# A mixer layer behind an in-projection: the units of the projection in another order, a 32x32 solve beside the last five of them, and one product in two halves

## The chip, the core and the metric

The kernel runs on one core of a Trainium2 chip. The metric is the time of one execution on the device in microseconds (us), median of several runs. The core's engines work from queues of their own and meet at semaphores: TensorE (PE) does matrix products into eight PSUM banks, VectorE (DVE) and ScalarE (ACT) do elementwise work and read PSUM, GpSimd (POOL) does elementwise work on SBUF, and SyncE (SP) issues the transfers. Each queue is worked through in order.

## The reference

Two blocks on 512 tokens of width 1024, all in float32. The first is a Fourier mix and a gated convolutional feed-forward. The second is a feed-forward, a mixer, and a feed-forward. The change lies in the mixer of the second block. Cut to it:

```python
p = rms_norm_2(x, mix_norm) @ w_in                    # 512 x 2208: r, k, v, w, a, g and 512 pooling inputs
p_rw = p_rw + (token_shift(p_rw) - p_rw) * mu_shift   # all but the pooling inputs
p_r, p_k, p_v, p_w, p_a, p_g = split(p_rw)
decay = exp(-exp(-softplus(-(w0 + tanh(p_w) @ w_lora_up)) - 0.5))
a = sigmoid(a0 + p_a @ a_lora_up)
g = sigmoid(p_g) @ g_lora_up
kk = p_k * k_k / norm_per_head(p_k * k_k)
k = p_k * (1 + (a - 1) * k_a)
# for each head (64 wide), one token after the other:
sa = state @ -kk
state = state * w + outer(sa, kk * a) + outer(v, k)
y = state @ r
y = group_norm(y) * ln_w + ln_b + sum(r * k * r_k) * v
out = concat([y * g, multiscale_pool_mix(p_pool)]) @ w_out
```

## The kernel before, in words

**Weights.** All large weights come as 233 units of 128x1024 floats through a ring of four slots. SP loads a unit into `raw`, ACT rounds it into `w_hi` (`high`, the copy at L623), POOL subtracts to get `w_lo` (`low`, four pieces of 128x256 at L459), and PE multiplies: eight blocks of three matmuls (`three`, L1568 to L1570), 24 for a unit.

**In-projection.** There are 18 units (`IN_ORDER`), 128 output channels each: `wa` (inputs of the decay and of `a`), `gx` (input of the gate), four of keys `k`, four of receptances `r`, four of values `v`, four of pooling inputs. Four PSUM banks are used in turn. Behind each unit PE does `small_products(i)`, DVE scales the bank into `pads` (`normed`), ACT takes its share of the token shift (`own_share`, L772) and DVE adds the other (`shifted`). Elementwise work on keys, decays and receptances is put by hand, by `if i == ...`, behind one unit or another in the four engines' programs. The names used below: `decay` (a scan and a subtraction), `key_sums` and `key_norms` (norms per head), `key_scale` and `key_unit` (the norms spread and applied), `removal(p)` (three DVE operations that make kk and kk*a with the decays in; p is one of four pairs of heads), `receptance(p)` (two), `triangle_grams(p)` (L1807, on PE, needs `removal(p)`), `tri_out(p)` (ACT copies the 32x32 diagonal blocks to `tri_g`, and others to `off`), `bonus_product` (L1813, needs `receptance`).

**The solve.** The recurrence is worked out in chunks of 64 tokens; that needs inverses of unit lower triangular 32x32 blocks, for all heads and chunks at once. `triangles()` on DVE is a generator: a transpose into `tri_m`, then 31 steps of a product into `tri_p` and an addition into `tri_x`, each waiting for the one before, then a transpose back into `tri_t`. `solve_steps(n)` issues n pieces of it (the first transpose is one).

**Pairs.** Two pairs of heads are worked at a time on two sets of buffers. `in_turns` writes the order: the even lane's first four pieces (up to `yield`), the odd lane's first four, ten more of the even lane, and then one of each in turn. A pair: four transposes (`tA` to `tV`, copied out by ACT), `LR` (masked by DVE at L1402), `K0` and `K1` (masked by DVE at L1407), `AV` (L1911, the masked keys times the values, copied out by ACT), then `G1` (L1922), `W` (L1929), `GH` (L1935) and more, and a scan `S1` to `S6` over the chunks (L1978 on PE, L1454 on DVE in turn). `G1` needs `TT`, four ACT copies of `tri_t` (L907), which stand in ACT's queue behind the copy of `AV`. PE's first transposes wait for `in_done`, which DVE gives at L1375, in its queue behind the solve steps of the in-projection.

## Time and profile before

| | us |
|---|---|
| median of 3 runs | 1612.47 (1611.6 to 1615.66) |
| the profiled execution, whole | 1617.07 |
| its span, first to last instruction | 1615.3 |
| busy in it: PE, POOL, DVE, ACT | 1509.5, 758.7, 560.2, 510.0 |

The in-projection takes the span from 880 to 1020 us, the pairs from 1022 to 1182. PE is busy for 93% of the span; the two stretches around 985 and from 1013 to 1060 us are those in this part where it is not. The granted clock of PE is given as a share of 2.4 GHz, and it has two levels, 1.2 and 2.4 GHz.

### The profile page before, as it was taken

Reading aid. Unit: us, or ns where it says so; the run is one execution under the profiler, and the core shown is the slowest. Engines: PE = TensorE matmul, PEld = TensorE weight load, DVE = VectorE, ACT = ScalarE, POOL = GpSimd, SP = SyncE. Lnnn points to the kernel's source line nnn. Section 1 sums busy time; section 2 is a strip of 40 time slices with the busy share of each in tenths; the row PEclk is TensorE's granted clock in tenths of the full one; section 3 lists DMA queues with packets and bytes.
Section 4 is the critical chain, followed back from the end, with each engine's and each line's share of the span. In section 5 each row is a group of like instructions: output and inputs, shape, how many; then the busy total and the mean of one; then the engine's idle time right before and its main releaser. Section 6 shows DMA issues by size and latency. Waiting matters only on the chain.

```text
span 1615.3 us, 20178 instructions
## 1 busy us (share of the span) xinstructions
PE 1509.5 (93%) x7230; PEld 1248.7 (77%) x7230; DVE 560.2 (35%) x790; ACT 510.0 (32%) x706; POOL 758.7 (47%) x1013
## 2 busy tenths in 40 slices
PE   5787999999999999999999999688888999999997
PEld 5675888888887788888887787577766888888887
DVE  6695342222004722222003546834434322222003
ACT  4424333333124332223124563122223323222212
POOL 0363464555555664455545544250025655445553
PEclk9888999999999999999999999779889999999999
DMA  8871234232231232322332221000012332232321
GB/s 308 313 261 40 92 131 147 100 100 96 92 103 65 92 117 91 104 91 92 103 101 69 95 79 40 1 1 1 1 53 91 105 104 91 91 104 92 103 78 53
DMA packets 44545, 156.90 MB, mean 97 GB/s; under 512 B 4944, under 2 KB 7376, under 8 KB 44240
## 3 DMA queue, kind: packets, MB, share of 16 engines
q1 hardware_dynamic: 44496, 156.22, 28.0%
q8 instruction: 33, 0.54, 0.1%
q14 instruction: 16, 0.13, 0.0%
HBM read 154.11 MB, written 2.10 MB: 97 GB/s over the span
## 4 chain that ended last, share of the span: by engine, by line
PE 81%; DVE 12%; ACT 3%; issue 3%; DMA 1%; POOL 1%; SPq 0%; DVEq 0%; ACTq 0%; POOLq 0%
PE ps L1568 24%; PE ps L1569 24%; PE ps L1570 24%; DVE mod_acc L1028 2%; DVE act_lo L1028 1%; PE ps L1922 1%; DVE hid_lo L1028 1%; PE ps L1911 1%; DVE tri_p L1025 1%; DVE tri_x L1025 1%; DVE xT L1028 1%; DVE MK L1407 1%; PE ps L1982 1%; PE ps L1581 1%; DVE act_lo L1025 1%
## 5 line engine op out<-in xcount | busy, mean ns | idle before, releaser
L459 POOL TENSOR_TENSOR w_lo<-raw,w_hi 128x256 fp32r<-128x256 f32 x932 | 692.7, 777 | 773.4 <-ACT w_hi L623 773.3
L1568 PE MATMUL ps<-act_hi,w_hi 128*128 128x512 f32 x1328 | 529.9, 399 | 19.2 <-DVE act_lo L1025 10.8
L1569 PE MATMUL ps<-act_lo,w_hi 128*128 128x512 f32 x1328 | 521.7, 393 | 0.0
L1570 PE MATMUL ps<-act_hi,w_lo 128*128 128x512 f32 x1328 | 520.9, 392 | 0.0
L623 ACT ACTIVATE w_hi<-raw 128x1024 fp32r<-128x1024 f32 x233 | 245.0, 1055 | 452.1 <-PE ps L1570 426.0
L1568 PEld LDWEIGHTS ps<-act_hi,w_hi 128*128 128x128 f32 x1328 | 252.3, 190 | 83.6 <-issue 13.5
L1569 PEld LDWEIGHTS ps<-act_lo,w_hi 128*128 128x128 f32 x1328 | 252.4, 190 | 53.5 <-issue 2.6
L1570 PEld LDWEIGHTS ps<-act_hi,w_lo 128*128 128x128 f32 x1328 | 252.2, 190 | 53.2
L1568 PE MATMUL ps<-hid_hi,w_hi 128*128 (+3 forms) x584 | 220.2, 377 | 10.8 <-DVE hid_lo L1028 7.3
L1569 PE MATMUL ps<-hid_lo,w_hi 128*128 (+3 forms) x584 | 219.6, 376 | 0.0
L1570 PE MATMUL ps<-hid_hi,w_lo 128*128 (+3 forms) x584 | 219.5, 376 | 0.0
L1568 PEld LDWEIGHTS ps<-hid_hi,w_hi 128*128 128x128 f32 x584 | 110.9, 190 | 31.0 <-issue 11.5
L1570 PEld LDWEIGHTS ps<-hid_hi,w_lo 128*128 128x128 f32 x584 | 110.9, 190 | 19.8
L1569 PEld LDWEIGHTS ps<-hid_lo,w_hi 128*128 128x128 f32 x584 | 110.9, 190 | 19.7
L718 ACT ACTIVATE hid_hi<-g_buf 128x512 f32 (+1 forms) x66 | 41.8, 633 | 257.9 <-DVE g_buf L1168 217.6
L1165 DVE TENSOR_TENSOR u_buf<-ps,rstd 128x512 f32<-128x512 f32 x44 | 30.4, 691 | 182.6 <-PE ps L1570 182.6
L1170 DVE TENSOR_TENSOR hid_lo<-g_buf,hid_hi 128x512 f32 (+1 forms) x66 | 48.2, 730 | 58.7 <-ACT hid_hi L718 58.7
L1163 DVE TENSOR_TENSOR g_buf<-ps,rstd 128x512 f32<-128x512 f32 x44 | 30.4, 691 | 93.9 <-PE ps L1570 93.5
L716 ACT ACTIVATE g_buf<-g_buf 128x512 f32<-128x512 f32 x66 | 41.1, 622 | 48.9 <-DVE g_buf L1155 37.3
L1153 DVE SCALAR_TENSOR_TENSOR g_buf<-ps,vec,g_buf 128x511 f32<-128x511 f32 x22 | 16.5, 750 | 106.6 <-ACT g_buf L714 106.6
L1028 DVE SCALAR_TENSOR_TENSOR xT<-ps,mods,xT 128x512 f32<-128x512 f32 x16 | 12.0, 751 | 115.9 <-PE ps L1570 115.5
L1533 DVE SCALAR_TENSOR_TENSOR xT<-ps,xT 128x256 f32<-128x256 f32 x16 | 6.8, 425 | 110.0 <-PE ps L1570 110.0
(262 smaller groups left out, 1175.0 us busy)
## 6 DMA issues: line engine op xcount, KB each, us to landing
raw<-weight_units SPq DMA_DIRECT2D x233, 512.0 KB, 3.2
wm_ring<-mod_units SPq DMA_DIRECT2D x16, 512.0 KB, 6.4
wm_mid<-mod_units SPq DMA_DIRECT2D x16, 512.0 KB, 7.1
wm_early<-mod_units SPq DMA_DIRECT2D x8, 512.0 KB, 9.5
wm_late<-mod_units SPq DMA_DIRECT2D x8, 512.0 KB, 5.3
x_tok<-tokens SPq DMA_DIRECT2D x4, 512.0 KB, 5.4
xT<-tokens_by_channel SPq DMA_DIRECT2D x1, 2048.0 KB, 16.4
result<-act_out SPq DMA_DIRECT2D x16, 128.0 KB, 1.8
```

The source lines that it names most:

```text
L459: ins = nc.gpsimd.tensor_tensor(w_lo[:, slot, c], raw[:, slot, c], w_hi[:, slot, c].bitcast(f32), SUB)
L623: nc.scalar.activation(w_hi[:, slot, :], raw[:, slot, :], ACT.Copy).then_inc(hi_done, 1)
L716: nc.scalar.activation(g_buf[:, q, :], g_buf[:, q, :], ACT.Silu).then_inc(s["silu"], 1)
L718: nc.scalar.activation(hid_hi[:, bass.ds(j * T, T)], g_buf[:, q, :], ACT.Copy).then_inc(s["hid_hi"], 1)
L1025: chain(nc.vector.tensor_tensor(o, a, b, op), name)
L1028: chain(nc.vector.scalar_tensor_tensor(o, a, s, b, op0, op1), name)
L1163: nc.vector.tensor_tensor(g, gate, rstd[:, :], MUL).then_inc(s["act_in"], 1)
L1165: nc.vector.tensor_tensor(u_, val, rstd[:, :], MUL).then_inc(s["val_read"], 1)
L1170: nc.vector.tensor_tensor(hid_lo[:, bass.ds(j * T, T)], g, hid_hi[:, bass.ds(j * T, T)].bitcast(f32), SUB).then_inc(s["hid_lo"], 1)
L1568: nc.tensor.matmul(o, wh, xh, start=start, stop=False, **check)
L1569: nc.tensor.matmul(o, wh, xl, start=False, stop=False, **check)
L1570: return nc.tensor.matmul(o, wl, xh, start=False, stop=stop, **check)
```

## The change

Four things move or are cut, and no operation is taken away:

1. `IN_ORDER` puts the four key units first, two value units, the receptances around one pooling unit, two value units, and three pooling units last. The small work follows: the grams stand behind units 10 and 11 (before, 12 and 13), the last receptances behind unit 13 (before, 17).
2. The solve's steps stand behind units 13 to 17 (5, 6, 6, 6, 6 pieces), and the rest in one piece ahead of pair 0's first mask. None is left between the masks of pairs 0 and 1.
3. `AV` becomes `AVa` (two chunks, needs only K0's masks) and `AVb` (needs K1's); ACT copies out the first half and DVE the second.
4. POOL's own order: `tri_x` is set up ahead of the low parts of units 12 to 14, the four products `key_in` stand ahead of those of units 15 to 17 (before, all low parts came first).

```diff
-IN_ORDER = [("wa", 0), ("gx", 0), ("k", 0), ("k", 1), ("pool", 0), ("k", 2), ("k", 3), ("pool", 1), ("r", 0), ("v", 0), ("r", 1), ("v", 1),
-            ("r", 2), ("v", 2), ("r", 3), ("v", 3), ("pool", 2), ("pool", 3)]
+IN_ORDER = [("wa", 0), ("gx", 0), ("k", 0), ("k", 1), ("k", 2), ("k", 3), ("v", 0), ("v", 1), ("r", 0), ("r", 1), ("pool", 0), ("r", 2),
+            ("r", 3), ("v", 2), ("v", 3), ("pool", 1), ("pool", 2), ("pool", 3)]
...
-            low_through(U_IN + AHEAD - 1, U_OUT)
+            low_through(U_IN + AHEAD - 1, U_IN + 12)
...
+            low_through(U_IN + 12, U_IN + 15)
             for p in range(PAIRS):
                 pool.wait_ge(sem("removed"), p + 1)
                 nc.gpsimd.tensor_tensor(rK[:, p, :], rBonus[:, p, :], rK[:, p, :], MUL).then_inc(sem("key_in"), 1)
+            low_through(U_IN + 15, U_OUT)
...
-                copy("AV", b.AA[:, :, :, HS:P], 2, "q (c h k) -> q c h k", c=NCP, h=2)
+                pe_did("AVa")
+                did("AVa", nc.scalar.activation(b.AA[:, 0:2, :, HS:P], ps[:, b.bank + 2, 0:HALF].rearrange("q (c h k) -> q c h k", c=2, h=2), ACT.Copy))
...
+                if i == 9:
+                    removal(0)
+                    removal(1)
                 if i == 10:
-                    for q in range(PAIRS):
-                        key_unit(q)
-                    removal(0)
-                if i == 11:
-                    removal(1)
+                    receptance(0)
                     removal(2)
+                    removal(3)
                 if i == 13:
-                    receptance(1)
-                if i == 14:
-                    solve_steps(4)
-                if i == 15:
+                    receptance(2)
+                    receptance(3)
+                    solve_steps(5)
+                if i >= 14:
                     solve_steps(6)
-                if i == 16:
-                    receptance(2)
-                    solve_steps(4)
-                if i == 17:
-                    receptance(3)
-                    solve_steps(4)
...
-                if p < 2:
-                    solve_steps(5)
                 if p == 0:
+                    solve_steps(SB)
                     for q in range(PAIRS):
                         bonus(q)
...
                 keys(0, 2)
-                if p < 2:
-                    solve_steps(2)
                 yield
                 keys(1, 0)
                 yield
+                pe_did("AVb")
+                did("AVb", nc.vector.tensor_copy(b.AA[:, 2:4, :, HS:P], ps[:, b.bank + 3, 0:HALF].rearrange("q (c h k) -> q c h k", c=2, h=2)))
                 yield
...
-                if i == 12:
+                if i == 10:
                     triangle_grams(0)
                     triangle_grams(1)
-                if i == 13:
+                if i == 11:
                     triangle_grams(2)
                     triangle_grams(3)
...
                 keys(1, 0)
+
+                def values(half):
+                    for c in (0, 1) if half == "a" else (2, 3):
+                        for h in range(2):
+                            last = nc.tensor.matmul(bank(2 + c // 2)[:, (c % 2 * 2 + h) * HS:(c % 2 * 2 + h + 1) * HS], b.MK[:, 1, c, h, :], b.VT[:, c * P + h * HS:c * P + (h + 1) * HS], start=True, stop=True)
+                    did(f"AV{half}", last)
+
+                ve_did("K0b")
+                values("a")
                 yield
                 ve_did("K1b")
-                for c in range(NCP):
-                    for h in range(2):
-                        last = nc.tensor.matmul(bank(2)[:, (2 * c + h) * HS:(2 * c + h + 1) * HS], b.MK[:, 1, c, h, :], b.VT[:, c * P + h * HS:c * P + (h + 1) * HS], start=True, stop=True)
-                did("AV", last)
+                values("b")
```

**DVE at the end of the in-projection and at pair 0.** First the kernel before, from solve step 20 on; `rBonus<-ps,rV` is `bonus`, `MBR` and `MK` are the masked `LR` and keys of pair 0.

```order
L1025 TENSOR_TENSOR tri_x<-tri_x,tri_p 128x10x22
L1025 TENSOR_TENSOR rBonus<-ps,rV 128x512 x4
L1402 TENSOR_TENSOR MBR_120<-ps,sumsq 128x4x128 x2
L1407 TENSOR_TENSOR MK_121<-ps,sumsq 128x2x2x128 x2
L1025 TENSOR_TENSOR tri_p<-tri_x,tri_m 128x207
L1025 TENSOR_TENSOR tri_x<-tri_x,tri_p 128x9x23
L1025 TENSOR_TENSOR tri_p<-tri_x,tri_m 128x192
L1025 TENSOR_TENSOR tri_x<-tri_x,tri_p 128x8x24
L1407 TENSOR_TENSOR MK_121<-ps,sumsq 128x2x2x128 x2
```

The changed kernel at the same place (its line numbers are one lower here, and ten lower further down):

```order
L1024 TENSOR_TENSOR tri_p<-tri_x,tri_m 128x31
L1024 TENSOR_TENSOR tri_x<-tri_x,tri_p 128x31
L1321 STREAM_TRANSPOSE tri_t<-tri_x 128x32x32
L1024 TENSOR_TENSOR rBonus<-ps,rV 128x512 x4
L1392 TENSOR_TENSOR MBR_120<-ps,sumsq 128x4x128 x2
L1397 TENSOR_TENSOR MK_121<-ps,sumsq 128x2x2x128 x4
L1406 COPY AA_119<-ps 128x4x64
L1392 TENSOR_TENSOR MBR_133<-ps,sumsq 128x4x128 x2
L1397 TENSOR_TENSOR MK_134<-ps,sumsq 128x2x2x128 x4
L1406 COPY AA_132<-ps 128x4x64
```

The whole solve, with its last transpose, now stands ahead of `bonus`; the masks of each pair stand together, and a copy of half of `AA` is new behind them.

**DVE around the grams' inputs.** The kernel before, from the shift of unit 10 (`rt`) on; three rows on `rAR`, `pk` and `rB` are one `removal`.

```order
L1028 SCALAR_TENSOR_TENSOR rt<-pads,vec,rt 128x512
L1028 SCALAR_TENSOR_TENSOR pk_90<-pk_90,vec,ps 128x512
L1028 SCALAR_TENSOR_TENSOR pk_91<-pk_91,vec,ps 128x512
L1028 SCALAR_TENSOR_TENSOR pk_92<-pk_92,vec,ps 128x512
L1028 SCALAR_TENSOR_TENSOR pk_93<-pk_93,vec,ps 128x512
L1028 SCALAR_TENSOR_TENSOR rAR<-pk_90,rAR 128x512
L1025 TENSOR_TENSOR pk_90<-pk_90,rB 128x512
L1025 TENSOR_TENSOR rB<-pk_90,rK 128x512
L1025 TENSOR_TENSOR pads<-ps,rstd 128x512
```

The changed kernel, from the last `key_unit` on, which stands ahead of unit 9's scaling:

```order
L1027 SCALAR_TENSOR_TENSOR pk_93<-pk_93,vec,ps 128x512
L1024 TENSOR_TENSOR pads<-ps,rstd 128x512
L1027 SCALAR_TENSOR_TENSOR rt<-pads,vec,rt 128x512
L1027 SCALAR_TENSOR_TENSOR rAR<-pk_90,rAR 128x512
L1024 TENSOR_TENSOR pk_90<-pk_90,rB 128x512
L1024 TENSOR_TENSOR rB<-pk_90,rK 128x512
L1027 SCALAR_TENSOR_TENSOR rAR<-pk_91,rAR 128x512
L1024 TENSOR_TENSOR pk_91<-pk_91,rB 128x512
L1024 TENSOR_TENSOR rB<-pk_91,rK 128x512
L1024 TENSOR_TENSOR pooled<-ps,rstd 128x512
```

The first two `removal`s now stand behind unit 9, where before they stood behind units 10 and 11.

**PE from K1 to G1 in pair 2**, with a scan step of pair 1 (`S_142`) between. Before:

```order
L1899 MATMUL ps<-rAR,rK 128x256 x4
L1978 MATMUL ps<-S_142,MT_139 128x128
L1911 MATMUL ps<-VT_124,MK_121 128x64 x8
L1978 MATMUL ps<-S_142,MT_139 128x128
L1922 MATMUL ps<-AA_119,TT_127 128x128 x8
```

And in the changed kernel:

```order
L1899 MATMUL ps<-VT_124,MK_121 128x64 x4
L1974 MATMUL ps<-S_142,MT_139 128x128
L1899 MATMUL ps<-VT_124,MK_121 128x64 x4
L1974 MATMUL ps<-S_142,MT_139 128x128
L1918 MATMUL ps<-AA_119,TT_127 128x128 x8
```

The first half of the value product has moved ahead of the scan step; the second stands where the whole one stood.

## Rows read from the trace of the kernel before

**Rows 1.** Waits of PE, 960 to 1150 us: us in total, times, longest.

```profile
PE ps L1922 <- ACT TT L907: 6.2, 3, 2.3
```

**Rows 2.** Timeline of PE, in-projection: start, us, what, count, idle before.

```profile
973.22 2.06 PE L1807 MATMUL ps<-rAR,rB 64*128 64x128 f32 x32
...
984.27 2.08 PE L1807 MATMUL ps<-rAR,rB 64*128 64x128 f32 x16 [3.33 <-ACT tri_g L823]
...
1001.48 0.79 PE L1568 MATMUL ps<-act_hi,w_hi 128*128 128x512 f32 x1
...
1012.82 1.02 PE L1813 MATMUL ps<-rkt,const 128*128 128x512 f32 x2
1017.92 2.07 PE L1813 MATMUL ps<-rkt,const 128*128 128x512 f32 x2 [4.08 <-DVE rkt L1028]
1022.40 1.11 PE L1884 MATMUL ps<-const,rAR 128*128 128x128 f32 x4 [2.41 <-DVEq L1375]
```

**Rows 3.** Timeline of DVE, 990 to 1050 us.

```profile
997.40 2.12 DVE L1311 STREAM_TRANSPOSE tri_m<-tri_g 128x1024 f32<-128x1024 f32 x1
999.55 0.91 DVE L1025 TENSOR_TENSOR tri_p<-tri_x,tri_m 128x31 f32<-128x31 f32 x1
...
1005.51 0.75 DVE L1028 SCALAR_TENSOR_TENSOR rV<-pads,vec,rV 128x512 f32<-128x512 f32 x1 [0.86 <-ACT rV L772]
...
1027.00 2.87 DVE L1025 TENSOR_TENSOR rBonus<-ps,rV 128x512 f32<-128x512 f32 x4
...
1047.52 1.95 DVE L1322 STREAM_TRANSPOSE tri_t<-tri_x 128x1024 f32<-128x1024 f32 x1
```

**Rows 4.** One tile, `tri_p`: duration in ns, min/median/max, first and last start.

```profile
L1025 DVE TENSOR_TENSOR tri_p<-tri_x,tri_m x31: 192/376/1216, 999.6 to 1045.9; 128x31 f32<-128x31 f32 x2, 128x60 f32<-128x60 f32 x2, 128x87 f32<-128x87 f32 x2, 128x112 f32<-128x112 f32 x2
```

**Rows 5.** Timelines of POOL and of DVE beside it, 970 to 980 us.

```profile
970.85 4.57 POOL L459 TENSOR_TENSOR w_lo<-raw,w_hi 128x256 fp32r<-128x256 f32 x4 [4.81 <-ACT w_hi L623]
971.44 1.11 DVE L1025 TENSOR_TENSOR pk<-pk,rB 128x512 f32<-128x512 f32 x1
...
978.18 0.69 DVE L1025 TENSOR_TENSOR pk<-pk,rB 128x512 f32<-128x512 f32 x1
```

**Rows 6.** The chain that ended last, 1029 to 1058 us: start, us, what.

```profile
1029.90 1.29 DVE MBR L1402 x2
...
1033.89 1.30 DVE MK L1407 x2
...
1035.23 3.68 PE ps L1911 x16
...
1042.96 1.29 DVE MBR L1402 x2
...
1053.44 3.78 PE ps L1922 x16
```

**Rows 7.** Timelines of PE, ACT and DVE together, pair 2, 1105 to 1116 us.

```profile
1105.42 1.28 DVE L1407 TENSOR_TENSOR MK<-ps,sumsq 128x512 f32<-128x512 f32 x2
1105.56 1.14 PE L1899 MATMUL ps<-rAR,rK 64*128 64x256 f32 x8
...
1108.21 2.00 PE L1911 MATMUL ps<-VT,MK 128*128 128x64 f32 x16 [0.71 <-DVE MK L1407]
...
1110.24 0.60 ACT L890 ACTIVATE AA<-ps 128x512 f32<-128x512 f32 x1 [6.76 <-PE ps L1911]
...
1110.74 1.68 ACT L907 ACTIVATE TT<-tri_t 32x256 f32<-32x256 f32 x4
1112.46 3.58 PE L1922 MATMUL ps<-AA,TT 128*128 128x128 f32 x16 [1.98 <-ACT TT L907]
```

**Rows 8.** Busy time of the engines in stretches: us, PE, PEld, DVE, ACT, POOL, PEclk, DMA share, GB/s.

```profile
984.27:988.62 4.35, 4.10 (x33) 3.61 (x33) 0.36 (x1) 4.23 (x10) 1.00 (x2) 0.50 0.02 4
...
1104.00:1110.20 6.20, 5.07 (x41) 3.86 (x38) 4.20 (x8) 0.00 (x0) 0.00 (x0) 1.00 0.01 3
1112.46:1115.80 3.34, 3.34 (x16) 3.34 (x17) 0.00 (x0) 0.60 (x1) 0.00 (x0) 0.54 0.00 0
```

More of the change, by code:

```diff
@@ L154, with in_turns @@
 AHEAD_OF_SOLVE = 4
-def in_turns(pair_program, closing, between=None):
+def in_turns(pair_program, closing):
     def lane(q):
@@ L168, in in_turns @@
             next(first)
-    if between is not None:
-        between()
     for _ in range(LAG):
@@ L829, in _ @@
                 name, p = IN_ORDER[i]
-                if i == 7:
-                    key_square(3)
+                if i == 3:
+                    decay_gates(0)
+                    decay_gates(1)
+                if i == 4:
+                    decay_gates(2)
+                    decay_gates(3)
+                if i == 5:
+                    gate_out(0)
+                    gate_out(1)
+                if i == 6:
+                    gate_out(2)
+                    gate_out(3)
+                    key_square(3)
+                if i == 7:
+                    key_norms()
+                    for q in range(PAIRS):
+                        widen(q)
+                if i == 11:
+                    tri_out(0)
+                    tri_out(1)
+                if i == 12:
+                    tri_out(2)
+                    tri_out(3)
                 if name != "pool":
@@ L842, in _ @@
                 if i == 4:
-                    decay_gates(0)
-                    decay_gates(1)
+                    for q in range(PAIRS):
+                        key_gain(q)
                     key_square(1)
                 if i == 5:
-                    decay_gates(2)
-                    decay_gates(3)
-                    for q in range(PAIRS):
-                        key_gain(q)
-                if i == 6:
                     key_square(2)
@@ L854, in _ @@
                     exponentials(1)
[L855 removed]
+                if i == 6:
                     exponentials(2)
                     exponentials(3)
[L858 to L874 removed]
             n_step = [0, 0]
@@ L1330, in _ @@
             for i, (name, p) in enumerate(IN_ORDER):
-                if name == "pool":
-                    pool_input(p)
-                else:
-                    normed(name, p)
-                    if i == 12:
-                        removal(3)
-                        receptance(0)
-                    shifted(name, p, {"wa": wa[:, 0, :], "gx": gx[:, 0, :], "k": pk[p], "r": rt[:, p % 2, :], "v": rV[:, p, :]}[name])
-                if i == 4:
+                if i == 3:
                     decay(0)
@@ L1377, in _ @@
             n_step = [0, 0]
-            def after_ahead():
-                solve_steps(SB)
             def pair(p):
@@ L1499, in closing @@
                 pool_lo(3)
-            in_turns(pair, closing, after_ahead)
+            in_turns(pair, closing)
             mix_lo(PAIRS - 1)
@@ L1920, in pair @@
                 for k, half in enumerate("ab"):
+                    if half == "b":
+                        ve_did("AVb")
                     for c, h, o in systems(half):
```

67 lines of the change are left out of this document (29 added, 38 removed).

## The prediction

> **What bounds the kernel now.** I read the page first: one core, the profiled execution 1617.07 us as a whole, 4.6 us above the median of 1612.47. I sum against the profiled execution and take the 4.6 off at the end. Everything outside the in-projection and the pairs keeps its code, so only 880 to 1182 us matters. There the waits of TensorE say that it stands 6.2 us in three waits for ACT's `TT` copies [rows 1]. Its timeline shows the other stands [rows 2]: 3.33 us ahead of the second lot of grams, 4.08 us for the last `rkt`, 2.41 us for DVE's `in_done`, whose queue is then full of solve steps. Last, the chain that ended last runs from 1029.90 to 1053.44 through DVE's masks of pairs 0 and 1, the value products and `TT` [rows 6]: 23.5 us for two pairs' masks. In that stretch the solve is the thread: its last transpose starts at 1047.52 [rows 3], and `G1` can't start before it. So the solve on DVE bounds this place, with TensorE waiting and, after each wait, at 1.2 GHz.
>
> **Part 1, the in-projection up to the grams.** The same products stand ahead of the first grams, but ten units instead of twelve. Two units took 11.34 us, products ahead of them excluded (1001.48 to 1012.82) [rows 2], 5.67 each. The first grams came at 973.22 [rows 2], so now they can come at 961.9. Their inputs are later than that: unit 9 ends one unit earlier, 956.3; its scaling, ACT's share and the shift take 2.3 us (0.7, the 0.86 of waiting, 0.75) [rows 3], to 958.6; then two `removal`s, six operations. They cost 0.69 alone and 1.11 beside POOL's low parts [rows 5]. ACT rounds unit 13 just then, so I take five of six slowed: 6.2 us, to 964.8 (4.4 us, 963.0, if none is). TensorE does the first grams alone (1.0 us), stands 1.9 us, and goes on slow: the grams and a unit's start after the 3.33 us stand ran at a granted clock of 0.50 [rows 2, 8], 1.2 GHz. That costs 1.0 on these grams and I estimate 1.6 on unit 11, which ends at about 974.2. The second grams find their inputs and `tri_read` there: the 3.33 us stand is gone. With them (2.0 us) and units 12 and 13 (11.3), unit 13 ends at 987.5.
>
> The GPSIMD Engine Reference of the Trainium skill (Specifications, SBUF interfaces) says that POOL contends with DVE instructions that have two SBUF inputs. The trace agrees, by the 1.11 and 0.69 us. By that rule alone all solve steps would be exposed too; they would be slowed only where POOL works.
>
> **Part 2, the solve.** Behind unit 13: scaling and shift 2.3 us, two `receptance`s of two operations (0.75 each with gaps [rows 3]) 3.0, and 1.1 for the low part of unit 17 beside them: 993.9. Then, ahead of `in_done`: the transpose, 2.15 [rows 3]; 28 of 31 steps. A step is a product and an addition; the median of a product is 0.376 us, the smallest 0.192 [rows 4], which by 31 pairs gives 23.3 us; my count from start to start along the timeline is 23.4, and the last three, the smallest but for the first, make 1.5 of it, so 21.9. One scaling and shift 2.3, three pooling scalings 2.2. Sum 28.6: `in_done` at 1022.5, where it was 1022.40 [rows 2]. TensorE, done with its units near 1013, simply waits longer in one piece; this wait takes the place of the 4.08 and the 2.41. Bounds: without slowed removals and without slow clock 4.5 us earlier; with the copies of the grams late or slowed steps 2 us later. In the kernel before, the first step took 0.91 for its product beside POOL's `key_in` [rows 3]; now `key_in` is done by 985, and only POOL's memsets are left beside the steps. I take 1022.5.
>
> **Part 3, pairs 0 and 1.** DVE goes on: three steps 1.5, the transpose 1.95, four `bonus` 2.87 [rows 3], so the first mask at 1028.9 (call it L) against 1029.90 [rows 6]. PE's transposes, ACT's copies, `LR` and `K0` go on beside this 6.4 us; before, they ended some 6.3 us behind 1022.40 by the timeline, so either could set L, within 0.2. From L on, relative to before [rows 6]: no solve steps between K0's and K1's masks, so K1's masks end at L+4.8 instead of 5.3; `AVa` follows K1's product at L+3.4 instead of the whole product at L+5.3; both halves (3.68 for the whole at 1.2 GHz) end at L+7.0 instead of 8.8. Pair 1's transposes and `LR` took from there to L+13.1 (1042.96); TensorE has now worked without a pause since L+1.3 and gets its full clock back within the transposes, so I take L+10.1. Then 1.2 and 1.2 for `LR` and K0's masks, K1's 1.3: L+13.8. `AVa` at L+12.6, 1.0 at full clock, copied at L+13.7. The copy of 128x256 has no row: it lies between 0.42 (one of four `TT` pieces) and 0.60 [rows 7]; I take 0.5. `TT` 1.68 [rows 7], and it no longer waits for the solve: `G1` at L+15.9 = 1044.8 against 1053.44 [rows 6]. That is **8.7 us earlier**. If the clock stays low, `AVa` takes 1.8 and it is 7.8.
>
> **Part 4, pairs 2 and 3.** Before, the whole value product waited for K1's masks (1108.21), took 2.0, ACT's copy 0.5 to the next, `TT` 1.7, and `G1` began at 1112.46 [rows 7]. Now `AVa` needs only K0's masks, which end at 1106.7 as K1's product does [rows 7]: 1.0, to 1107.8; copy from 1108.0, `TT` from 1108.4, `G1` at 1110.1: 2.4 us earlier. DVE's new copy of the second half waits for `AVb` at 1109.3 and ends by 1109.8, inside `TT`. So 2.4 each for pairs 2 and 3, which repeat the pattern. And the clock: it was 1.00 from 1104 to 1110.2 and 0.54 behind the 1.98 us stand [rows 8], in which `G1` took 3.58 us [rows 7]; at the full clock eight such products in two passes would take about 2.2. The stand shrinks to some 0.4 us; the 0.71 ahead of the value product was followed by no loss. So I add 1.3 each: **3.7 us** a pair, 7.4 in all, and 4.8 without the clock.
>
> TensorE: Matmul & The Clock Gate of the Trainium skill (Part 1) says that the slow clock is the default and sustained activity releases it, and that waits in the middle of a kernel bring it back. The rows agree in direction. By that rule a stretch whose stand is taken out keeps the full clock, which is the 7.4; if the clock falls all the same, it is 4.8.
>
> POOL: low parts of units 12 to 14 now wait behind `tri_x` (the norms at 951), those of 15 to 17 behind `key_in` (about 970 to 977). They then need 2.8 to 4.6 us [rows 5]; unit 12 starts at 976, unit 15 near 993. Hidden, with 10 us over.
>
> **Sum.** 8.7 + 7.4 = 16.1 us off 1617.07 is 1601.0; less 4.6, 1596.4. I say 1596.5.
>
> **The rivals.**
> (a) *The likeliest*, as summed: 11 to 20 us less, 1592.5 to 1601.5. Chance 0.64.
> (b) *The grams' inputs are in time*: the removals not slowed, no slow clock at unit 11, and `G1` of pair 0 at full clock too. `in_done` 4.5 us earlier and 1.4 on `G1`: 22 us less, 1590.5. For it: TensorE has few stands there. Against: ACT rounds a unit exactly behind unit 9's share. 0.12.
> (c) *The wait moves to `in_done`*: DVE holds all 28 steps ahead of `in_done`, where before it held 18. If steps are slowed or ACT's `tri_out` comes late, `in_done` slips; each us costs one. With 6 us of slip and no gain of clock: 8.7 - 6 + 4.8 = 7.5 less, 1605. For it: DVE has nearly no idle time from 988 on, so nothing absorbs a slip. 0.13.
> (d) *It does nothing*: the pairs' scans, which take turns on DVE and TensorE, come to bound pairs 2 and 3, so that AV's 7.4 falls away, and `in_done` slips 5 us: 4 less, 1608.5 to 1617. Against: scan step 5 waited behind `G1`, not the other way. 0.07.
> (e) *Slower*: POOL's queue. `key_in` waits for the fourth `removal`; unit 15's low part is behind it. If that removal came over 10 us after the 975 I expect, unit 15, and with it the solve, would slip one for one; from 27 us after on, the kernel is slower. No row points there. 0.04.
>
> **How the numbers follow.** What a measurement of this kernel can tell from no change is about 0.3%, 4.8 us. Faster by more: (a), (b), (c) 0.89, less a little of (c): 0.88. Within: 0.08. Slower: 0.04. The range takes (a), most of (b) down to 1588.5, and the nearer part of (c) up to 1603.5.
>
> **What would show it.** Right: no stand ahead of the second grams; one of about 2 us between the first two lots; one wait of 8 to 10 us for DVE's queue ahead of the transposes at 1022.5; first mask near 1029, `G1` of pair 0 near 1045; the three waits for `TT`, 6.2 us now, under 3 in all; granted clock near 1 in `G1` of pairs 2 and 3. Wrong: transposes later than 1026 (the solve slowed, or unit 13 late), `G1` of pairs 2 and 3 still at 0.5, or a wait of TensorE for `w_lo` at unit 15.

## The result, and the profile after

Beside runs of the kernel before on the same chip, the changed kernel took 1593.88 us (median of 4, 1588.5 to 1597.47) against 1612.32 (median of 4): ratio 0.9887, with a 95% interval of 0.9866 to 0.9908. That is 18.4 us less, 14.8 to 21.6 by the interval. A second set on another chip gave 1590.6 against 1612.23, ratio 0.9875 (0.9854 to 0.9896). The forecast was 1596.5, range 1588.5 to 1603.5. A few single executions ran far longer than the rest (1753, 3049 and 3857 us of the kernel before, 5275 us of experiment 6); the ratios leave them out.

TensorE's waits from 870 to 1175 us in the changed kernel (line waited with, releaser: us in total, times, longest):

```profile
PE ps L1872 <- DVEq L1369: 10.3, 1, 10.3
...
PE ps L1918 <- ACT TT L906: 1.3, 3, 0.7
```

The 6.2 us of waits for `TT` [rows 1] are 1.3. The stands ahead of the last `rkt` and of `in_done` [rows 2] are one wait of 10.3 us for VectorE's queue, and the 3.33 us ahead of the second lot of grams are gone.

TensorE's timeline (start, us, operation, count, idle before in brackets), first the in-projection and pair 0:

```profile
962.10 1.16 PE L1797 MATMUL ps<-rAR,rB 64*128 64x128 f32 x16
965.50 1.16 PE L1797 MATMUL ps<-rAR,rB 64*128 64x128 f32 x16 [2.24 <-DVE rB L1024]
...
967.96 0.63 PE L1558 MATMUL ps<-act_hi,w_hi 128*128 128x512 f32 x1
...
971.04 0.39 PE L1558 MATMUL ps<-act_hi,w_hi 128*128 128x512 f32 x1
...
973.87 1.16 PE L1797 MATMUL ps<-rAR,rB 64*128 64x128 f32 x16
975.70 1.16 PE L1797 MATMUL ps<-rAR,rB 64*128 64x128 f32 x16 [0.67 <-DVE rB L1024]
...
1023.66 1.12 PE L1872 MATMUL ps<-const,rAR 128*128 128x128 f32 x4 [10.34 <-DVEq L1369]
...
1031.48 1.13 PE L1887 MATMUL ps<-rAR,rK 64*128 64x256 f32 x8 [1.79 <-DVE MBR L1392]
1032.68 1.10 PE L1899 MATMUL ps<-VT,MK 128*128 128x64 f32 x8
...
1034.95 0.61 PE L1872 MATMUL ps<-const,rAR 128*128 128x128 f32 x4
...
1043.69 2.05 PE L1918 MATMUL ps<-AA,TT 128*128 128x128 f32 x16 [0.72 <-ACT TT L906]
```

And the last pair:

```profile
1123.63 2.05 PE L1918 MATMUL ps<-AA,TT 128*128 128x128 f32 x16 [0.31 <-ACT TT L906]
```

The first grams come where they were expected, with a stand of 2.24 us between the first two lots. Both lots took 1.16 us for 16 products, the full clock, where the forecast had half. The clock fell a little later: the first eight products of unit 11 started 0.43 us apart (0.63 each in the rows), the later ones 0.23 (0.39). The second grams also have a stand inside, 0.67 us. Pair 0's first grams (line 1918, `G1`) start at 1043.69 (expected 1044.8, before 1053.44 [rows 6]), and the last pair's at 1123.63 and at full clock: 2.05 us, where pair 2's took 3.58 before [rows 7].

VectorE in the same stretch:

```profile
968.43 1.65 DVE L1027 SCALAR_TENSOR_TENSOR rAR<-pk,rAR 128x512 f32<-128x512 f32 x1
970.12 1.67 DVE L1024 TENSOR_TENSOR pk<-pk,rB 128x512 f32<-128x512 f32 x1
...
973.27 1.65 DVE L1024 TENSOR_TENSOR pk<-pk,rB 128x512 f32<-128x512 f32 x1
...
996.82 0.21 DVE L1024 TENSOR_TENSOR tri_p<-tri_x,tri_m 128x31 f32<-128x31 f32 x1
...
1025.23 1.98 DVE L1321 STREAM_TRANSPOSE tri_t<-tri_x 128x1024 f32<-128x1024 f32 x1
...
1030.14 1.29 DVE L1392 TENSOR_TENSOR MBR<-ps,sumsq 128x512 f32<-128x512 f32 x2
...
1035.15 0.42 DVE L1406 COPY AA<-ps 128x256 f32<-128x256 f32 x1 [1.20 <-PE ps L1899]
```

and GpSimd beside it, at its `key_in` products:

```profile
967.82 3.42 POOL L528 TENSOR_TENSOR rK<-rBonus,rK 128x512 f32<-128x512 f32 x2
972.59 1.78 POOL L528 TENSOR_TENSOR rK<-rBonus,rK 128x512 f32<-128x512 f32 x1 [1.35 <-DVE rB L1024]
```

Removals 2 and 3 are slower than was reckoned: three of six operations took 1.65 to 1.67 us, each beside GpSimd's products. The first step's product takes 0.21, where it took 0.91 beside GpSimd [rows 3]. The last transpose now ends at 1027.21, 16 us ahead of `G1`; before it stood at 1047.52 [rows 3].

### The profile page after: what moved, and what is told of

Read it like the earlier page. It is cut to its first block, busy times and chain, and to the rows that moved or that the text cites. A ratio compares the mean times of both kernels' runs of the same rounds, so it can differ in the third digit from the quotient of the medians.

```text
span 1595.7 us, 20172 instructions
## 1 busy us (share of the span) xinstructions
PE 1499.1 (94%) x7230; PEld 1237.9 (78%) x7230; DVE 565.7 (35%) x794; ACT 508.6 (32%) x706; POOL 761.8 (48%) x1013
## 4 chain that ended last, share of the span: by engine, by line
PE 77%; issue 11%; DVE 7%; POOL 4%; ACT 1%; DVEq 0%; POOLq 0%; ACTq 0%
PE ps L1558 23%; PE ps L1560 23%; PE ps L1559 23%; POOL w_lo L457 4%; DVE act_lo L1027 1%; DVE tri_p L1024 1%; DVE tri_x L1024 1%; PE ps L1918 1%; DVE xT L1027 1%; PE ps L1978 1%; DVE mid_sq L1027 0%; PE ps L1925 0%; PE ps L1931 0%; PE ps L1974 0%; PE ps L1965 0%
```

## The experiments

All ratios are to the kernel before on the same chip, with 95% intervals. Since profiled executions of one kernel proved to differ (below), I read each profile in four stretches between marks on TensorE: from the start to pair 0's first transposes (T0), from there to `G1` of pair 0, from there to `G1` of pair 3, and from there to the end of the span. L is the first mask, as in the prediction. U is the first product of the in-projection, ahead of which no kernel differs; it came between 873.6 and 879.9 us, and that spread is in the first column but not in U-T0. Even U-T0 is rough: from U to the first grams, nine profiles of one order took 81.1 to 84.4 us. All in us, differences of starts in the timelines:

```
kernel                     start-T0    U-T0   T0-G1(0)  G1(0)-G1(3)  G1(3)-end   L-G1(0)
before                       1022.4   142.5     31.0       91.4        470.5       23.5
before, second profile       1021.4   143.2     31.2       89.5        471.1       23.5
split alone                  1019.5   144.8     29.6       81.7        467.2       22.0
solve placed as before       1019.4   140.4     29.3       84.7        467.1       22.0
changed, products whole      1019.3   142.6     26.8       89.9        471.6       20.4
the same, second profile     1017.2   142.6     26.8       90.3        471.1       20.4
changed                      1023.7   144.4     20.0       79.9        472.1       13.6
changed, second profile      1019.1   144.3     20.0       80.6        465.0       13.6
GpSimd's old order           1023.0   146.7     20.0       82.5        466.9       13.6
early release                1021.2   141.5     28.7       84.0        467.1       18.0
early release and tail       1019.8   141.5     23.6       80.8        466.3       16.3
all four edits               1014.2   137.4     20.9       79.8        465.2       13.6
two edits in the gaps        1021.7   143.4     20.0       79.8        468.1       13.6
early transpose              1017.4   143.8     20.0       79.4        465.1       13.6
```

**1. Value products whole again** (the rest as changed).

```diff
-                ve_did("K0b")
-                values("a")
                 yield
                 ve_did("K1b")
-                values("b")
+                for c in range(NCP):
+                    for h in range(2):
+                        last = nc.tensor.matmul(bank(2)[:, ...], b.MK[:, 1, c, h, :], b.VT[:, ...], start=True, stop=True)
+                did("AV", last)
```

> The changed kernel with part 4 undone: the value products of a pair again in one group behind the last key mask, copied by one 128x512 copy on ScalarE; the rest as changed. Theory (the copy and the triangle copy behind it on ScalarE hold up the first grams of a pair): each of pairs 2 and 3 is longer by 2.4 to 3.7 us, pairs 0 and 1 together by 0 to 4, so 5 to 9 us above the changed kernel, and the first grams of each pair wait for ScalarE's triangle copy by some 2 to 3 us again. Rival (the undivided copy is hidden by the lag between two pairs, and what was won there came only from the clock after the earlier start): within 2 us of the changed kernel.

Measured: 1613.4 us (median of 12), ratio 0.999 (0.9975 to 1.0005): as the kernel before, and 17 to 19 us above the changed one by the ratios where 5 to 9 were expected. Nothing of the gain is left that a median can show, although the solve's new place is still there. The twelve times lie in two lots, five from 1606.3 to 1609.4 and seven from 1612.9 to 1616.0. TensorE's timeline of this kernel, pair 0 and the last pair:

```profile
1027.09 1.13 PE L1884 MATMUL ps<-rAR,rK 64*128 64x256 f32 x8 [2.26 <-DVE MBR L1391]
1029.61 3.67 PE L1896 MATMUL ps<-VT,MK 128*128 128x64 f32 x16 [1.39 <-DVE MK L1396]
...
1033.08 1.06 PE L1869 MATMUL ps<-const,rAR 128*128 128x128 f32 x4
...
1041.57 2.29 PE L1896 MATMUL ps<-VT,MK 128*128 128x64 f32 x16 [1.39 <-DVE MK L1396]
1046.12 3.78 PE L1907 MATMUL ps<-AA,TT 128*128 128x128 f32 x16 [2.26 <-ACT TT L905]
...
1126.59 1.16 PE L1877 MATMUL ps<-rAR,rB 64*128 64x128 f32 x16
...
1136.04 3.78 PE L1907 MATMUL ps<-AA,TT 128*128 128x128 f32 x16 [1.98 <-ACT TT L905]
...
1146.65 1.95 PE L1920 MATMUL ps<-AA,TT 128*128 128x128 f32 x16
```

and the last pair with the products divided (the kernel of experiment 2):

```profile
1123.85 1.16 PE L1895 MATMUL ps<-rAR,rB 64*128 64x128 f32 x16
...
1127.60 1.10 PE L1914 MATMUL ps<-VT,MK 128*128 128x64 f32 x8
...
1130.75 2.05 PE L1933 MATMUL ps<-AA,TT 128*128 128x128 f32 x16 [0.31 <-ACT TT L908]
...
1136.85 1.95 PE L1946 MATMUL ps<-AA,TT 128*128 128x128 f32 x16
```

Busy time and granted clock (PEclk) between the start of `G1` and that of the second use of `TT` (`GH`), here of the whole products:

```profile
1136.04:1146.65 10.61, 10.61 (x49) 10.13 (x50) 2.17 (x4) 1.19 (x2) 0.00 (x0) 0.55 0.00 0
```

and of the divided ones:

```profile
1130.75:1136.85 6.10, 6.10 (x49) 5.62 (x50) 2.30 (x5) 1.19 (x2) 0.00 (x0) 1.00 0.00 0
```

The stand ahead of `G1` is 1.98 us here and 0.31 there, 1.67 apart. But `G1` takes 3.78 against 2.05, and `GH` (the last row of each) begins 10.6 us behind the start of `G1` against 6.1. TensorE is busy without a gap for all of both stretches, with 49 products in each; only the clock differs, 0.55 and 1.00. So the stand costs 1.7 us and what runs at half clock behind it 4.5 in this pair. From pair 3's `LR` to its `G1` the two kernels differ by 2.55 us (9.45 and 6.90), close to the 2.4 expected; the rest lies behind `G1`, where the forecast had put only 1.3.

In pair 0 the whole products cost 6.8 us from L to `G1`, in three places. They wait 1.39 us for K1's masks and take 3.67 us at half clock (1.10 and 1.10 in the changed kernel), so that pair 1's transposes come 2.5 us later against L. These run at half clock, 1.6 us more. The last 2.7 lie ahead of `G1`, behind pair 1's second key products.

**2. The split alone**, put into the kernel before (the same edit the other way round).

> The kernel before with part 4 alone: value products in two halves, nothing else. Theory: 5 to 8 us below the kernel before, about 2.4 to 3.7 for each of pairs 2 and 3 and some 0 to 2 in pairs 0 and 1, where the start of the first pair is set by VectorE's masks and its own clock. Rival (the gain of the two parts is one and the same, the end of a wait that the solve leaves): under 2 us below the kernel before. Together with the run that undoes part 4 it says whether the parts add up: if they do, the two differences are equal within the measurement.

Measured: 1601.11 us, ratio 0.9928 (0.9912 to 0.9944): 11.6 us less by the ratio (9.0 to 14.2), where 5 to 8 were expected. The stretch from `G1(0)` to `G1(3)` is 7.8 to 9.7 us shorter than in the two profiles of before, the end 3.3 to 3.9. In pair 0 it brought little, 1.5 us from L on. VectorE's timeline there:

```profile
1045.40 1.92 DVE L1323 STREAM_TRANSPOSE tri_t<-tri_x 128x1024 f32<-128x1024 f32 x1
```

ScalarE's:

```profile
1047.36 1.69 ACT L908 ACTIVATE TT<-tri_t 32x256 f32<-32x256 f32 x4 [4.44 <-DVE tri_t L1323]
```

TensorE's:

```profile
1049.10 3.78 PE L1933 MATMUL ps<-AA,TT 128*128 128x128 f32 x16 [4.08 <-ACT TT L908]
```

The last transpose of the solve stands behind pair 1's masks and its new copy, ScalarE's copy of `TT` waits 4.44 us for it, and `G1` 4.08 us for that, then at half clock. The parts don't add up: 11.6 alone, 17 to 19 on top of the rest. By their intervals the two figures could lie closer together; the plainer evidence is pair 0's 1.5 us here against 6.8 in experiment 1.

**3. Solve placed as before**, with the new order and the divided products kept.

```diff
                 if i == 13:
                     receptance(2)
                     receptance(3)
-                    solve_steps(5)
                 if i >= 14:
-                    solve_steps(6)
+                    solve_steps(6 if i == 15 else 4)
...
+                if p < 2:
+                    solve_steps(5)
                 if p == 0:
-                    solve_steps(SB)
                     for q in range(PAIRS):
                         bonus(q)
...
                 keys(0, 2)
+                if p < 2:
+                    solve_steps(2)
...
-            in_turns(pair, closing)
+            in_turns(pair, closing, lambda: solve_steps(SB))
```

> The changed kernel with the solve's VectorE steps placed as in the kernel before (4, 6, 4 and 4 steps behind the last units, the bonus and the rest of the steps around the masks of pairs 0 and 1, the last transpose between the pairs); the order of the in-projection and the divided value products as changed. Theory (the solve that stood among the masks is what the change takes away): the first grams of pair 0 come 7 to 11 us later against the first mask than in the changed kernel, and the whole is 7 to 12 us above it, so 6 to 11 below the kernel before. Rival (the three stands of the in-projection, 3.3, 4.1 and 2.4 us, that the new order takes away are the gain, and the place of the solve costs the same wherever it stands): within 3 us of the changed kernel.

Measured: 1597.6 us, ratio 0.9897 (0.9882 to 0.9912), so 16.6 us below the kernel before; the changed kernel's two ratios are 1.6 and 3.5 us lower, with intervals that overlap. The medians differ by 3.7 and 7.0. In the profile `G1` comes 22.0 us behind the first mask against 13.6: the 7 to 11 expected there were 8.4. The stretch to T0 is some 5 us shorter against the first grams (56.1 against 61.5), since the steps are not ahead of it, and pays that back. What is left is 2 to 7 us, less than the 7 to 12 expected, and by the overlapping intervals not told from nothing.

Experiments 1 to 3 side by side show how pair 0 works. From the first mask to `G1`: 23.5 us before, 20.4 with only the solve out of the way, 22.0 with only the products divided, 13.6 with both. Each alone leaves one stand ahead of `G1` (2.26 for the whole copy, 4.08 for the last transpose), and `G1` at 3.78 us behind it.

**4. GpSimd's old order** (all low parts ahead of the unit diagonal and of `key_in`).

```diff
-            low_through(U_IN + AHEAD - 1, U_IN + 12)
+            low_through(U_IN + AHEAD - 1, U_OUT)
...
-            low_through(U_IN + 12, U_IN + 15)
             for p in range(PAIRS):
                 pool.wait_ge(sem("removed"), p + 1)
                 nc.gpsimd.tensor_tensor(rK[:, p, :], rBonus[:, p, :], rK[:, p, :], MUL).then_inc(sem("key_in"), 1)
-            low_through(U_IN + 15, U_OUT)
```

> The changed kernel with GpSimd's old order: all low parts of the in-projection ahead of the unit diagonal of the solve's input and of the products that feed it. Theory (GpSimd has room, and its new order only lets the solve's first steps begin earlier, beside the last units): the first steps move back by what the last four low parts take, up to some 5 us; they had been ahead of a 10 us wait of TensorE that VectorE sets, so 0 to 5 us above the changed kernel, 2 likeliest. Rival (the low parts set TensorE's pace, and the split of them had been costly): the kernel is 1 to 3 us faster than the changed one.

Measured: 1592.27 us, ratio 0.9864 (0.9846 to 0.9881), not told from the changed kernel's 0.9887 and 0.9875. In the profile this part of the change is worth 2.4 us all the same: TensorE's wait for `in_done` was 13.7 us instead of 10.3 (1.0 of this because its units were done earlier), and T0 came 63.9 us behind the first grams instead of 61.5 (that it stands at 1023.0 is due to an earlier start of the in-projection). The `key_in` products now stand beside the solve's first steps, and four operations there took 0.82 to 1.22 us instead of 0.21 and 0.22:

```profile
993.70 1.21 DVE L1022 TENSOR_TENSOR tri_x<-tri_x,tri_p 128x31 f32<-128x31 f32 x1
994.94 1.22 DVE L1022 TENSOR_TENSOR tri_p<-tri_x,tri_m 128x60 f32<-128x60 f32 x1
```

Removals 2 and 3 ran at 0.69 us an operation in exchange. The 2.4 us lie within what was expected (0 to 5, 2 likeliest), and are too few for the times to show.

**5. The changed kernel again.** No edit.

> The changed kernel once more, unchanged, beside the three that follow. What it settles: how far two profiled executions of one kernel differ. Theory: the first grams of the four pairs come at the same times within 1 us, and the 472.1 us from the last pair's first grams to the end of the span are 467 to 468 here, as in the three runs with divided value products on another chip, because TensorE keeps 2.4 GHz behind 1158 us; then the changed kernel's own time is nearer 1592. Rival: 472 again, so that the 5 us belong to the changed kernel.

Measured: 1590.6 us, ratio 0.9875 (0.9854 to 0.9896). Its profiled execution was the fastest, a span of 1584.7 us against 1595.7 in the first profile, 11 us for one program. TensorE's timeline of the second profile:

```profile
957.54 1.16 PE L1797 MATMUL ps<-rAR,rB 64*128 64x128 f32 x16
...
1019.05 1.12 PE L1872 MATMUL ps<-const,rAR 128*128 128x128 f32 x4 [10.34 <-DVEq L1369]
...
1039.07 2.05 PE L1918 MATMUL ps<-AA,TT 128*128 128x128 f32 x16 [0.71 <-ACT TT L906]
```

and both profiles in stretches (us, PE, PEld, DVE, ACT, POOL, PEclk, DMA share, GB/s), of the first profile:

```profile
100.00:200.00 100.00, 85.99 (x357) 67.19 (x356) 56.82 (x64) 37.77 (x51) 43.83 (x52) 0.90 0.29 104
...
1165.00:1210.00 45.00, 41.10 (x155) 32.84 (x154) 10.71 (x15) 10.90 (x15) 17.96 (x24) 0.81 0.19 62
```

and of the second:

```profile
100.00:200.00 100.00, 87.08 (x375) 68.12 (x375) 61.90 (x67) 37.62 (x51) 45.55 (x52) 0.93 0.29 105
...
1165.00:1210.00 45.00, 41.26 (x174) 33.34 (x172) 13.45 (x19) 14.51 (x20) 20.96 (x27) 0.96 0.25 82
```

From the first grams to T0 both take 61.5 us, from there to `G1(3)` 100.0 and 100.6. They differ ahead, by 4.6 us (4.5 of it ahead of the in-projection; granted clock 0.90 and 0.93 from 100 to 200 us, a stage that the change doesn't touch), and behind `G1(3)`, by 7.1 (clock 0.81 and 0.96 from 1165 to 1210). So the 472.1 us of the first profile do not belong to the changed kernel; the stretch was 465.0 to 468.1 in all nine other profiles with divided products, and 470.5 to 471.6 in all four with whole ones. My expectation of the same times within 1 us held only from mark to mark.

**6. Early release.** `in_done` ahead of the last six steps.

```diff
+                if i == len(IN_ORDER) - 1:
+                    after(unit_used, U_OUT)
+                    ve.sem_inc(sem("in_done"), 1)
                 if i >= 14:
                     solve_steps(6)
-            after(unit_used, U_OUT)
-            ve.sem_inc(sem("in_done"), 1)
```

> The changed kernel with the release of the pair stage given ahead of the last six solve steps and not behind them, so that TensorE's 10.3 us wait is shorter by some 4.4. Theory (VectorE, not that wait, sets the first mask; the products were there 0.4 us ahead of it): the first mask stays at 1030 and the time within 1 us of the changed kernel; only the clock could gain or lose. Rival (TensorE's longest wait is worth its length): 3 to 4 us faster. A second rival: the masks' products are then followed by a longer stand of TensorE, the clock falls before the first grams, and the kernel is 2 to 4 us slower.

Measured: 1601.4 us, ratio 0.9926 (0.9904 to 0.9949), some 8 us slower than the changed kernel by the ratio on the same chip, 0.9875, whose interval lies clear of it. The second rival held, and its price was more than the 2 to 4 us given. TensorE's timeline:

```profile
1021.16 1.11 PE L1873 MATMUL ps<-const,rAR 128*128 128x128 f32 x4 [5.98 <-DVEq L1367]
...
1033.27 2.08 PE L1888 MATMUL ps<-rAR,rK 64*128 64x256 f32 x8 [5.57 <-DVE MBR L1393]
1035.28 3.67 PE L1900 MATMUL ps<-VT,MK 128*128 128x64 f32 x16
...
1049.88 3.17 PE L1919 MATMUL ps<-AA,TT 128*128 128x128 f32 x16 [0.72 <-ACT TT L906]
```

The wait for `in_done` is shorter by 4.4 us, as meant, and a stand of 5.57 us ahead of K1's products takes its place. Behind it K1 takes 2.08 us (1.13 in the changed kernel), the value products 3.67 for all 16 and pair 1's transposes 1.06 (0.61). From L to `G1` that is 18.0 us instead of 13.6, and 3.8 us more from there to `G1(3)` than the mean of the two profiles of the changed kernel gives (84.0 and 80.3). A wait of 10.3 us ahead of work that is not on the path was free; the same wait in two pieces, one of them on the path, cost half a per cent.

**7. Early release, and the solve's tail behind pair 0's masks.**

```diff
                 if p == 0:
-                    solve_steps(SB)
                     for q in range(PAIRS):
                         bonus(q)
...
                 keys(1, 0)
+                if p == 0:
+                    solve_steps(3)
...
+        if between is not None:
+            between()
...
-            in_turns(pair, closing)
+            in_turns(pair, closing, lambda: solve_steps(SB))
```

`between` runs behind pair 0's first four pieces and so ahead of pair 1's masks; it gives what is left of the solve.

> As the run with the early release, and besides it the last steps of the solve behind the first pair's masks: three steps in the 1.2 us in which VectorE waits for the first pair's second half of value products, the rest and the last transpose in the 2.4 us ahead of the second pair's masks. Theory (VectorE is the bound from 990 to 1040, and work of it moved into its own waits comes off the path): 2 to 4 us below the changed kernel. Rival (the last transpose then reaches the triangle copy on ScalarE late, as in the kernel before): within 1 us of the changed kernel or above it, with a wait of 2 us or more of the first grams of pair 0 for that copy.

Measured: 1592.57 us, ratio 0.9886 (0.9862 to 0.991): as the changed kernel, not 2 to 4 us below. From the first grams to `G1(0)` it took 80.8 us against 81.5 and 81.6. The rival's result came about, but not by its wait, for `G1` waited 0.71 us for `TT`, as before:

```profile
1028.40 1.88 PE L1891 MATMUL ps<-rAR,rK 64*128 64x256 f32 x8 [2.13 <-DVE MBR L1394]
1030.21 3.67 PE L1903 MATMUL ps<-VT,MK 128*128 128x64 f32 x16
...
1043.36 2.05 PE L1922 MATMUL ps<-AA,TT 128*128 128x128 f32 x16 [0.71 <-ACT TT L908]
```

The first mask comes 3.6 us earlier against the first grams. But the stand ahead of K1 is 2.13 us (1.79 in the changed kernel), K1 and the value products run at half clock again, and from L to `G1` it takes 16.3 us instead of 13.6: 2.7 of the 3.6 go there.

**8. All four edits**: these two, and two in VectorE's waits for TensorE.

```diff
                     for q in range(PAIRS):
                         key_unit(q)
+                    removal(0)
...
                 if i == 9:
-                    removal(0)
                     removal(1)
...
+                if i == 12:
+                    solve_steps(1)
                 if i == 13:
                     receptance(2)
                     receptance(3)
-                    solve_steps(5)
+                    solve_steps(4)
```

> The early release and the tail of the solve behind the first masks, and two edits more: the first removal ahead of the product of receptance 0, in VectorE's 3.6 us wait for TensorE, which should end the 2.2 us stand at the first grams; and the first transpose of the solve in the 3.1 us wait ahead of the next-to-last product unit of the values, ahead of the last two receptances and not behind them. Theory: 2.2 us from the stand, 2.1 from the transpose, 2 to 4 from the tail, so 6 to 8 us below the changed kernel. Rival (VectorE's waits in the in-projection are TensorE's pace, and what is put there only moves): no more than the run with the tail alone.

Measured: 1588.91 us, ratio 0.9863 (0.9838 to 0.9888). By the ratio 2 to 4 us below the changed kernel, by intervals that overlap; 6 to 8 were expected. **9. Only the two edits in the gaps:**

> The changed kernel with only the two edits in VectorE's waits for TensorE (the first removal ahead of receptance 0's product, the solve's first transpose ahead of the last two receptances); the release of the pair stage and the tail of the solve stay as changed. Theory (VectorE is the bound from the removals to the first masks, so work put into its waits shortens the path; the tail behind the masks brought nothing by itself): 2 to 4 us below the changed kernel, 1586 to 1589, not above the run with all edits. Rival (the gain of that run came from the early release together with the tail): as the changed kernel, within 1 us.

Measured: 1591.37 us, ratio 0.9854 (0.9832 to 0.9876). **10. Only the early transpose:**

> The changed kernel with one edit: the solve's first transpose in VectorE's 3.1 us wait ahead of the last two receptances. Theory: the transpose of 2.1 us comes off the path, the pair stage is released 2.1 us earlier against the first grams of the in-projection than in the changed kernel, and the time is 1 to 2 us below it. Rival (TensorE's units set the pace to the end of the in-projection): no change, with VectorE waiting 2 us longer elsewhere.

Measured: 1587.53 us, ratio 0.9854 (0.9827 to 0.9881). TensorE's first grams and T0 in it:

```profile
957.78 1.16 PE L1799 MATMUL ps<-rAR,rB 64*128 64x128 f32 x16
...
1017.43 1.12 PE L1874 MATMUL ps<-const,rAR 128*128 128x128 f32 x4 [8.46 <-DVEq L1371]
```

They lie 59.65 us apart against 61.5 in the changed kernel: 1.9 us shorter, nearly the 2.1 us of the transpose. The three kernels with it lie 2 to 5 us below the changed kernel by their ratios, and no interval parts them from it. It is the best candidate, and not shown to be faster than the changed kernel; faster than the kernel before it is. The first removal's move brought nothing further that the times can show (0.9854 both with and without it).

**11. The kernel before, and 12. the whole products, once more**, for their profiles.

> The kernel before, unchanged, for a second profile. Theory (the profile of before was of a late execution: 1617 against a median of 1612 to 1613): the pair stage from its first transposes to the last pair's first grams takes 122 us within 1.5 again, the tail behind them 467 to 472, and the start comes 3 to 4 us earlier. Rival: the same 1022 us for the start, so that the changed order and the divided value products alone would also have to be explained ahead of that point.

> The changed kernel with undivided value products, unchanged, for a second profile. Theory (the runs of this kernel lie in two lots, near 1607 and near 1613, and the first profile fell in the lower): the pair stage from its first transposes to the last pair's first grams is 117 us again in the one lot and 120 to 123 in the other, where a stand of TensorE is followed by half clock. Rival: the two lots differ ahead of the pair stage.

Their rows stand in the table. T0 to `G1(3)` of before was 122.4 and 120.7 us, of the whole products 116.8 and 117.1. The start of before was 1.0 us earlier, not 3 to 4, so a late start was only a small part of its 4.6 us above the median. Both profiles of the whole products are of executions in the lower of its two lots, at 1607.23 and 1609.36 us; what the executions from 1612.9 us on do differently is in no profile, and stays open.

## Why the prediction was right, step by step

**In sum** it was right: 16.1 us were summed, and 18.4 measured, 14.8 to 21.6. Case (a), 11 to 20 less, came true; the second set, 20.2 less, lies at its edge, and of (b) it has `G1` of pair 0 at full clock. **In its parts** it was right where it named the places and wrong in two sizes and in how they combine.

- *Part 1.* First grams expected ready at 964.8 and found at 965.45, the stand 1.9 and 2.24 us: right. Of the 2.6 us for the slow clock 1.6 came, all of it in unit 11 and none in the grams: from the start of the second lot to unit 11's last product it took 8.05 us, where the second grams' last lot and unit 12 took 6.48 at full clock. The 1.0 us that didn't come made up for a start 0.7 us later (965.50), and the second grams began at 973.87 where 974.2 was expected. Then came a stand of 0.67 us among them that the sum did not have: they wait for removals 2 and 3, which took 7.2 us for six operations beside `key_in`, and no row of before had shown the 1.65. Unit 13 was to end at 987.5, and the products behind it start at 987.86: small misses that nearly cancelled.
- *Part 2.* From the first grams to `in_done` 60.6 us were expected (961.9 to 1022.5), and 61.5 to 61.6 measured in the four profiles with these parts as they are. Behind the start of the in-projection T0 comes at 144.3 and 144.4 us, before at 142.5 and 143.2, so it stayed within what such profiles scatter by. Rival (c), a slip of 6 us, didn't occur. The stands of 3.33, 4.08 and 2.41 us brought nothing by themselves in this kernel, because the ten more solve steps ahead of `in_done` took their place; with these steps left behind (experiment 3) T0 comes at 140.4. The new order's use is to make room for the solve beside the units.
- *Part 3.* L to `G1(0)` expected 15.9 us, measured 13.6, because TensorE kept its full clock from K1's products on (1.13 us for 8), which I had given it only from pair 1's transposes on. The 8.7 us became 10.0 from L on. The text names the solve as what bounds this place, and gives no share of the 8.7 to the divided products that it sums beside it. Experiments 1 and 2 show that the solve's place alone brings 3.1 and the division alone 1.5, and only both 10.0. This is the weak step: "`TT` ... no longer waits for the solve" is true, but with whole products the value products first wait 1.39 us for K1's masks, the clock falls there, and `G1` waits another 2.26 for `TT` behind ScalarE's copy.
- *Part 4.* The 2.4 us to `G1` of pairs 2 and 3 was 2.55 in pair 3, between experiments 1 and 2 (shown). The term for the clock, 1.3 each, was the mis-sized one: I counted `G1` alone. What follows it up to `GH` runs slow too: from the start of `G1` to that of `GH` the whole products took 4.5 us more in pair 3, and 2.4 in pair 2 (7.8 and 5.4). In the whole kernel the division alone was worth 11.6 us (9.0 to 14.2), 1.5 of it in pair 0, where 7.4 stood for pairs 2 and 3.
- *GpSimd*'s low parts were hidden, as said. Its new order was worth 2.4 us ahead of `in_done` by the profile (experiment 4), because `key_in` is done before the solve's first steps; the times can't show it.

So the sum came out near because the parts it changed were all changed together: part 3 needs both the solve's place and the division, and part 4 was set too low by some 3 to 5 us. Undone one by one, by the ratios: division alone 11.6; new order beside it some 5 (16.6 less 11.6, and the two intervals touch at 0.9912); the solve's place on top of both 2 to 7, and not told from nothing; new order and solve's place without the division 1.6 or nothing (-0.8 to 4.0). What I can't settle is how much of the last figure is chance: the profiles show 3.6 to 5.6 us saved between T0 and `G1(3)` in that kernel, the median of 12 none.

TensorE: Matmul & The Clock Gate of the Trainium skill (Part 1) says that waits in the middle of a kernel bring the slow clock back. The traces agree for the stands of 1.92 us and more ahead of `G1` (`G1` took 3.49 to 3.79 us behind every one of them) and for the 2.24 us at the first grams, behind which the clock fell in all nine profiles of that order, but not for the 2.50 us ahead of K1 in experiment 8, where it stayed at 1.00.

## What to carry to other kernels

Price a stand of TensorE on the path with what runs behind it at half clock until the full clock is back: here 1.7 us of waiting cost another 2.4 in one pair and 4.5 in the other. Two stands in a row are one problem: in pair 0 either part alone took 1.5 or 3.1 us off and both together 10.0. So test a change of two parts by undoing each: here the division was worth 11.6 us alone and 17 to 19 beside the rest. Let a long wait stay in one piece ahead of work that is not on the path; giving the release earlier moved it onto the path and cost 8 us. And compare profiles from mark to mark, since two executions of one program differed by 11 us in stretches that the change did not touch. Where a program's times lie in two lots, a profile speaks only for its own lot.

## What the runs showed of the hardware

- The granted clock doesn't follow from the length of the last stand alone. It was at half behind stands of 1.98 us (`G1`, 3.78), 2.13 (K1, 1.88 for 8 products, experiment 7) and 5.57 (2.08). It stayed at 1.00, until 1042 us, behind the 2.50 ahead of K1 in experiment 8:

```profile
1022.79 1.13 PE L1893 MATMUL ps<-rAR,rK 64*128 64x256 f32 x8 [2.50 <-DVE MBR L1396]
```

- A fall can come a little behind the stand. Behind the 2.24 us at the first grams it came up to some 1.7 us later, in the next unit (1.16 for the lot of grams), or at once, as in experiment 1:

```profile
961.16 2.07 PE L1794 MATMUL ps<-rAR,rB 64*128 64x128 f32 x16 [2.24 <-DVE rB L1023]
```

  The price was the same either way: from this lot's start to the unit's last product 7.94 to 8.06 us in nine profiles, 1.6 more than at full clock. Short stands in a row do it too: behind one of 0.97 us and five of 0.44 between scan steps, pair 1's `G1` ran at half clock in the changed kernel (3.62 us) as in the kernel before, and in no run here was it under 2.9.
- VectorE's 128x512 operations on two tiles in memory took 0.69 us alone, 1.10 beside GpSimd's low parts and 1.65 beside its 128x512 products (`key_in`, two in 3.42). The short operations of the solve's first steps took 0.21 alone and up to 1.22 beside those products: about 1 us more in either case.
- Copies of 128x256 out of the accumulators took 0.38 us on ScalarE and 0.42 on VectorE, both below the 0.5 that I had taken between 0.42 and 0.60.
- The first grams of one and the same order came between 955.7 and 964.0 us in nine profiles; the clock from 100 to 200 us was 0.88 to 0.90 in the four where they came from 962 on, and 0.91 to 0.95 in the five where they came earlier.
